# Forgetting attention in a streaming encoder layer: another order of the keys' transposes and of two kinds of copies

## The reference

```python
c = jnp.cumsum(lf_all, axis=1)                       # running sum of log forget gates
s = einsum('bqhd,bkhd->bhqk', q_blk, k_all) * dh ** -0.5
s = where(mask, s + (c_q - c_k), -inf)               # causal, per frame
p = softmax(s, axis=-1)
o = einsum('bhqk,bkhd->bqhd', p, v_all)
```

## Time and profile before

| | us |
|---|---|
| median of 3 runs | 1683.87 |
| lowest, highest | 1683.22, 1684.84 |
| the profiled execution's own time | 1684.58 |
| its span, first to last instruction | 1682.8 |
| TensorE matmuls busy | 1653.3 |
| VectorE, ScalarE, GpSimd busy | 1082.6, 776.9, 319.0 |

### The profile page before, as it was taken

The page is one execution under the profiler, slowest core; times in us unless marked ns, Lnnn a source line. Parts: engine busy times, 40 slices in busy tenths (PEclk is TensorE's granted clock), DMA queues, the critical chain, the costliest instruction groups (busy, mean ns, idle before and its releaser), DMA issues.

```text
span 1682.8 us, 27461 instructions
## 1 busy us (share of the span) xinstructions
PE 1653.3 (98%) x9540; PEld 1490.5 (89%) x9540; DVE 1082.6 (64%) x2322; ACT 776.9 (46%) x1632; POOL 319.0 (19%) x486
## 2 busy tenths in 40 slices
PE   8999999999999999999999999999999999999998
PEld 8999999999889988889988899888888888888886
DVE  7556666543889744454445597888887668774744
ACT  6477777765777633352233433222222334443521
POOL 1311111115333321134532230000000000000242
PEclk9999999999999999999999999999999999999999
DMA  5221212231222455463443422444432764444541
GB/s 187 77 61 42 76 47 59 73 104 38 63 66 67 145 188 167 160 210 123 146 138 113 128 91 92 132 143 143 143 130 105 253 222 113 129 151 125 192 162 75
DMA packets 164315, 205.35 MB, mean 122 GB/s; under 512 B 16152, under 2 KB 113240, under 8 KB 164208
## 3 DMA queue, kind: packets, MB, share of 16 engines
q1 hardware_dynamic: 164208, 203.97, 37.8%
HBM read 144.85 MB, written 57.28 MB: 120 GB/s over the span
## 4 chain that ended last, share of the span: by engine, by line
PE 79%; DVE 8%; issue 4%; ACT 4%; POOL 2%; DMA 1%; SPq 0%; ACTq 0%; DVEq 0%; POOLq 0%
PE gb L501 9%; PE gb L2285 5%; PE sc L3168 5%; PE gb L3168 5%; PE gb L2820 4%; PE gb L2656 4%; PE sc L2820 4%; PE tp L3168 4%; PE tp L2820 4%; PE tp L796 3%; PE gb L928 3%; PE gb L929 3%; PE gb L930 3%; PE sc L2444 3%; PE tp L2444 3%
## 5 line engine op out<-in xcount | busy, mean ns | idle before, releaser
L928 PE MATMUL gb<-Xh,wh 128*128 128x384 f32 (+1 forms) x504 | 176.0, 349 | 0.0
L929 PE MATMUL gb<-Xh,wl 128*128 128x384 f32 (+1 forms) x504 | 170.7, 339 | 0.0
L930 PE MATMUL gb<-Xl,wh 128*128 128x384 f32 (+1 forms) x504 | 170.7, 339 | 0.0
L487 POOL TENSOR_TENSOR wl<-raw,wh 128x256 fp32r<-128x256 f32 x168 | 125.7, 780 | 236.7 <-ACT wh L472 175.7
L3292 POOL TENSOR_TENSOR wl<-raw,wh 128x1024 fp32r<-128x1024 f32 x2 | 5.3, 2632 | 559.8 <-ACT wh L3283 559.8
L501 PE MATMUL gb<-Xh,wh 128*128 128x384 f32 (+1 forms) x288 | 103.9, 361 | 0.0
L501 PE MATMUL gb<-Xh,wl 128*128 128x384 f32 (+1 forms) x288 | 97.4, 338 | 0.0
L501 PE MATMUL gb<-Xl,wh 128*128 128x384 f32 (+1 forms) x288 | 97.3, 338 | 0.0
L928 PEld LDWEIGHTS gb<-Xh,wh 128*128 128x128 f32 x504 | 95.0, 189 | 0.1
L796 PE MATMUL tp<-ident,u 128*128 128x128 f32 x536 | 85.2, 277 | 10.0 <-DVE u L1670 6.9
L929 PEld LDWEIGHTS gb<-Xh,wl 128*128 128x128 f32 x504 | 95.0, 188 | 0.0
(11 more groups left out here) (546 smaller groups left out, 4769.5 us busy)
## 6 DMA issues: line engine op xcount, KB each, us to landing
zr<-u_scr SPq DMA_DIRECT2D x91, 256.0 KB, 2.9
raw<-in_w_in SPq DMA_DIRECT2D x70, 256.0 KB, 3.2
u_scr<-ustore SPq DMA_DIRECT2D x26, 576.0 KB, 3.6
u_scr<-ustore SPq DMA_DIRECT2D x13, 768.0 KB, 3.2
sig_scr<-sig SPq DMA_DIRECT2D x16, 576.0 KB, 3.1
raw<-in_w_up SPq DMA_DIRECT2D x36, 256.0 KB, 4.4
kc<-in_cache_fox_k SPq DMA_DIRECT2D x8, 1024.0 KB, 5.6
vc<-in_cache_fox_v SPq DMA_DIRECT2D x8, 1024.0 KB, 7.8
```

The costliest lines, as they stand in the source:

```text
L487: nc.gpsimd.tensor_tensor(wl[U.slot][:, q], raw[U.slot][:, q], wh[U.slot][:, q].bitcast(F32), ALU.subtract).then_inc(w_lo if x == 3 else w ...
L928: nc.tensor.matmul(gb[c][:, 0:x1 - x0], wh[U.slot][:, ws], Xh3[:, k, x0:x1], start=(k == 0), stop=False)
L929: nc.tensor.matmul(gb[c][:, 0:x1 - x0], wl[U.slot][:, ws], Xh3[:, k, x0:x1], start=False, stop=False)
L930: last = nc.tensor.matmul(gb[c][:, 0:x1 - x0], wh[U.slot][:, ws], Xl3[:, k, x0:x1], start=False, stop=(k == KT - 1))
```

## The change

In `fox_pe` the keys' round at t = 5, 6, 7 is issued behind two more filling units in place of behind all of them. In `fox_act` the third values' round's copies (t = 4) stand ahead of that step's exponential, and all rounds' copies stand ahead of the keys' split. In `fox_dve` the copies of finished chunks of keys and values are made in the step after the one in which the chunk ends, behind its minimum pass and low halves. Numbers of instructions, operands, tiles and the numbering of the rounds stay as they are.

```diff
--- before.py
+++ after.py
@@ -1309,9 +1309,12 @@
                     fill_pe(pe, FOX_FILL, FOX_FILL_UNITS, s, at_, m)
                     at_ = m
                     v_round_pe(pe, p, t - 2)
+                if p < 4 and t in (5, 6, 7):
+                    m = min(at_ + 2, fill)
+                    fill_pe(pe, FOX_FILL, FOX_FILL_UNITS, s, at_, m)
+                    at_ = m
+                    k_round_pe(pe, p, t - 5)
                 fill_pe(pe, FOX_FILL, FOX_FILL_UNITS, s, at_, fill)
-                if p < 4 and t in (5, 6, 7):
-                    k_round_pe(pe, p, t - 5)
 
         def fox_act(act):
 
@@ -1330,14 +1333,16 @@
                         rope_act(act, Unit(m), c, c, 1.0)
                 for m, x in FOX_HI[s]:
                     hi_half(act, Unit(m), x)
+                if p < 4 and t == 4:
+                    v_round_act(act, p, 2)
                 if s < ITEMS:
                     fox_exp_act(act, s)
-                if s % 8 == 5 and (s + 3) // 8 < 8:
-                    k_split_act(act, (s + 3) // 8)
-                if p < 4 and t in (2, 3, 4):
+                if p < 4 and t in (2, 3):
                     v_round_act(act, p, t - 2)
                 if p < 4 and t in (5, 6, 7):
                     k_round_act(act, p, t - 5)
+                if s % 8 == 5 and (s + 3) // 8 < 8:
+                    k_split_act(act, (s + 3) // 8)
                 if s % 4 in (1, 2) and (s + 3) // 4 < 16:
                     q_split_act(act, (s + 3) // 4, s % 4 - 1)
                 for m, c in FOX_ENDS[s]:
@@ -1374,6 +1379,10 @@
                 for m, c in FOX_ENDS[s - 1] if s else ():
                     if m == U_KB:
                         rope_k_dve(v, c)
+                    elif m in (u_v(1), u_v(2), u_v(3)):
+                        v_keep(v, m, c, (m - 1) // 3)
+                    elif m in (u_k(1), u_k(2), u_k(3)):
+                        k_keep(v, m, c, (m - 1) // 3)
                 M = (s + 2) // 4
                 if s % 4 == 2 and M < 16:
                     v.wait_ge(q_hi, 2 * M + 1)
@@ -1391,10 +1400,6 @@
                 for m, c in FOX_ENDS[s]:
                     if m == U_KB and c == 2:
                         rope_k_dve(v, c)
-                    elif m in (u_v(1), u_v(2), u_v(3)):
-                        v_keep(v, m, c, (m - 1) // 3)
-                    elif m in (u_k(1), u_k(2), u_k(3)):
-                        k_keep(v, m, c, (m - 1) // 3)
 
         def fox_keep_pool(pool, p, m, sem_, dst, src, sign):
 
```

## The result

The changed kernel takes 1687.60 us (median of 10 runs, 1686.37 to 1689.04), the one before 1684.03 (10 runs, 1683.22 to 1684.84): +3.6 us. The two medians divide to 1.0021; the ratio on record for all the runs is 1.0019, with a 95% interval of 1.0011 to 1.0027. Forecast were 1686.8 and, from the median then known, +2.95. The sign is clear of the noise, and the size lies on the line of 0.2% that the forecast drew between "same" and "slower".

The account below looks back on a forecast made before the run. TensorE's matmuls, busy 98% of the span, were taken to set the time. Terms 2.9 - 1.2 - 1.35 + 1.2 + 1.4 = +2.95 us took the median from 1683.87 to 1686.8, range 1683.6 to 1690.0.

Parts of the forecast that it names:

- part 1: Keys' rounds inside the filling (t = 5, 6, 7): TensorE waits for turn 0's bank; cost 0.7 a period, 2.9 us.
- part 3: Third values' copies ahead of the exponential on ScalarE (t = 4): 0.35 gained a period, 1.2 us in four.
- Part 2: Keys' copy ahead of the split on ScalarE (t = 5): no cost; margin for next turn copy 0.1 to 0.3 us.
- Part 4: VectorE's projection copies behind next minimum pass and low halves: t = 15 gains 1.35, t = 8 costs 1.2, t = 0 costs 1.4.
- A: The forecast itself: 1686.8 us, own range 1685.4 to 1688.6; chance 0.52.
- B's first form: Keys' rounds' waits cost full length, no drain hidden: 4.4 in place of 2.9, 1688.3 us; B's chance 0.26 covers both forms.
- second form: Of B: late reciprocal uses up its margin, holding turn copy and VectorE's low half: 1690 to 1692 us; shares chance 0.26.
- C: Losses from VectorE's moved projection copies are absorbed, as later keys' rounds leave VectorE time: 1684.2 us; chance 0.12.
- D: Keys' round inside the filling finds its bank free, no waits: sum -5.9, so 1678 us; chance 0.10.

Follow-up runs that it names:

- e1_keys_only: Kernel before with only the keys' rounds at t = 5, 6, 7 moved inside the filling, all copies as before: 1687.41 us, ratio 1.0017.
- e2_no_keys_in_fill: Changed kernel with the keys' rounds put back behind all of the filling, copies still reordered: 1687.92 us, ratio 1.0017 to the kernel before.
- e7_keys_one_later: Changed kernel with the keys' round one filling unit later (three units ahead of it, not two): 1685.31 us, ratio 1.0009 to the kernel before.
- e4_values_only: Kernel before with only the third values' round's copies (t = 4) moved ahead of the exponential: 1682.55 us, ratio 0.9987.
- e3_copies_only: Kernel before with only VectorE's copies of finished key and value chunks moved into the next step: 1685.68 us, ratio 1.0004.
- e9_split_early: e8_all_values_first with the keys' split of t = 5 made at t = 1 and the keys' rounds behind up to four filling units: 1678.53 us, ratio 0.9966.
- e8_all_values_first: Kernel before with all three values' rounds' copies ahead of the exponential and the t = 15 copy behind the next minimum pass: 1680.45 us, ratio 0.9981.

## Why the prediction was right, point by point

The forecast's own likeliest case (1685.4 to 1688.6) holds the measured 1687.6. No step of it failed in kind; one term, part 1, was too small. By its steps, read in the second period:

| step | forecast us | measured us |
|---|---|---|
| waits of the keys' round, t = 5, 6, 7 | 1.05, 1.02, 0.48 | 1.04, 1.03, 0.47 |
| cost of part 1 at t = 5, 6, 7 | 0.21, 0.4, 0.1 | 0.25, 0.43, 0.11 |
| part 3, a period | -0.35 | -0.36 |
| hole at the third scores chunk, t = 15 | 0.8 to 0.35 | 0.80 to 0.33 |
| hole at the third turn, t = 9 and t = 1 | 0.5 and 0.6 | 0.52 and 0.62 |
| stage, sum | +2.95 | +3.38 |

**Part 1** was right in place and mechanism, and its term was too small: 0.79 against 0.72 us in the second period, and more over all four. By the first minimum passes of t = 5 and t = 8 the changed kernel loses 0.93, 0.82, 0.79 and 0.83 us there, together 3.37 against 2.9. The first period, which the forecast took to be like the second, costs most; why was not tried. e1_keys_only shows the part alone, at 3.45. The drain (the end of the matmuls in front, which a wait hides) was rightly counted, for without it the forecast had 1.1 a period.

**Part 2** cost nothing in the changed kernel, by e1_keys_only, which has the other order and the same waits. But the margin that the forecast gave as 0.1 to 0.3 us is what decides in e2_no_keys_in_fill and e7_keys_one_later, where the keys' transposes come later and the copy holds up the split. Taking the order back gains 1.35 us in e7_keys_one_later. In these kernels the order is a risk without a return.

**Part 3** is the one part that pays by itself, 1.29 us in e4_values_only against 1.2.

**Part 4** has one move that pays (t = 15) and two that cost, as forecast; e3_copies_only shows +1.44 where the three terms of the forecast make 1.25. The rule of the Trainium skill that the forecast weighed (VectorE: DVE Perf Modes, The DRAIN you can't avoid) would have added 0.08 a copy: here the copy starts at 188.12, 0.09 before the low half in front of it has ended at 188.21, so the rows again do not bear it out for this pair. The same section adds that an operation that is not held starts earlier, which the forecast left out. The copy starts with no idle time in front of it, and the rows fit that case.

**The sum.** e1, e3 and e4 add up to 3.45 + 1.44 - 1.29 = 3.60, and the changed kernel has 3.38: parts 1, 3 and 4 are nearly independent. Part 2 is not, for it costs nothing beside part 1 and some 3.7 us without it. The forecast fell short by 0.43 us, and by the first minimum passes that is all part 1 (3.37 against 2.9). Parts 3 and 4 come to -1.26 and +1.27 there, against -1.2 and +1.25.

**Behind the stage.** The forecast let the stage's difference go through to the end. The profiled executions differ by 2.4 us in place of 3.4. The waits of weight loads from 400 to 600 us, in the sliding-window stage, first before, then after:

```profile
PEld tp L796 <- DVE u L1670: 11.4, 15, 1.6
```

```profile
PEld tp L796 <- DVE u L1675: 10.7, 17, 1.4
```

They differ by 0.7 us with no change to that code, and over the twelve kernels here this row lies between 10.4 and 12.1. So a profiled span tells such a small change to about 1 us, and the median of ten runs (+3.6) agrees with the stage. Why that stage's waits vary was not tried.

**The rivals.** A came. B's first form, no hidden drain, did not: part 1 cost 0.84 a period on average and not 1.1. Its second form was seen in other kernels. C did not: neither costly copy was absorbed. D did not come either: all 12 rounds found their bank taken. Where the round's place is later and the split is out of its way, e9_split_early, the two edits together gain 2.0 us. The other 3.6 of that kernel's 5.6 us come from the values' copies and the move at t = 15.

## What to carry to other kernels

Before a piece of work is moved earlier on the engine that sets the time, look up what frees its buffer, and where that release stands in the same step: here the round moved 1 us ahead of the low half that frees its bank, and each of the three holes above came back as a longer one in front. Place it near the point where the bank becomes free, and take away what delays its reader (the split in front of its copy) by moving that to a step in which it holds up nothing (here t = 1).

A copy that fills an idle stretch ahead of a wait is free, and the same copy behind the wait is in the chain. Judge such moves one by one: of six moved copies, one paid, two cost and three did nothing.

## What the runs showed of the hardware

That weight loads behind a wait run closer than unhindered ones was used in the forecast, and the keys' four transposes show it again: 0.42 us behind a wait (169.69, changed kernel), 0.54 without one (167.01, e9_split_early). It cuts both ways: closing a hole of 0.4 us before five transposes (e8_all_values_first) stretched them from 0.53 to 0.65 us, so that part of a closed hole does not come back.
